# Long convolution: inputs turned by VectorE in 32x32 blocks, first input stage as products on 32x64 tiles

## The chip, the cores and the metric

The kernel runs on one core of a Trainium2 chip. The metric is the device time of one execution in microseconds (us). Engines are named as in the profile: PE is TensorE (PEld its weight loads), DVE is VectorE, ACT is ScalarE, POOL is GpSimd, SP is SyncE.

## The reference

Two blocks over a sequence of 2048 tokens with 1024 channels. The first is banded attention with multi-scale pooling. The second mixes a gated long convolution (changed here) with a spatial gating unit:

```
def second_block(x, ...):
    h = rms_norm(x, pre_norm_w); proj = h @ w_in
    hy_in, hy_gate, sg_u, sg_v, sg_gate = split(proj)
    x0, x1, v = split(short_conv_centred(hy_in, conv_w, conv_b))
    k = hyena_filter(L, ...)                      # (2L, 1024), divided by its l1 norm
    y_a = x0 * long_conv_bidir(v * x1, k, hyena_skip) * silu(hy_gate)
    ...
def long_conv_bidir(u, k, skip):
    U = rfft(u, n=2 * L, axis=1); K = rfft(k, axis=0)
    return irfft(U * K, n=2 * L, axis=1)[:, :L] + u * skip
```

Each channel's 2048 samples are thus convolved with a filter of 4096 taps and gated.

## The kernel before

The FFT of length 4096 is done in two stages of 64 points each, as matrix products, on two groups of 128 channels at a time: a chunk `cc` (four of them) is 256 channels, a group `ug` (eight) is 128 channels, `ug = 2*cc` or `2*cc + 1`. Everything lies in `long_convolution`, which is one program for each engine; the engines meet by semaphores alone, and each runs its instructions in the written order.

Filter: `generate(kq)` on PE makes 1/16 of a chunk's filter, `weighted(kq)` on DVE multiplies it by the decay, `absolute` (ACT) and `summed` (DVE) build the l1 norm. `filter_first(cc)` multiplies by the first-stage matrix in 16 groups, four PSUM banks in turn (0 to 3), and `filter_turned` (DVE) turns each out of PSUM.

Inputs: `channels_in(ug)` (SP) loads a group into UIN, channels on partitions, time along the row. Before, `inputs_turn(ug)` on PE transposes it in 16 steps of 128x128 into banks 0 and 1, `inputs_out(ug)` on ACT copies these to UI in four steps, and `inputs_first(ug)` on PE makes eight products of 128x128 by 512 columns, two for each of four groups of channels `g`, into banks 0 and 1 for even `g` and 2 and 3 for odd; `inputs_turned(ug)` on DVE turns them, 1024 columns at a time, into the buffer UB (`UTC`).

Loop: `second_stage(cc)` takes 16 steps `p`. In each, PE forms the second stage of filter and inputs, ACT copies the filter's form, DVE makes three products and a difference (the complex product), PE does `inverse(n)`, ACT writes it back into UB, and PE and DVE generate and weight a sixteenth of the next chunk's filter.

Boundary, between two loops: PE does `filter_first(cc+1)`, `inputs_turn(2cc+2)`, `inverse_first(2cc)`, `inputs_first(2cc+2)`, `inputs_turn(2cc+3)`, `inverse_first(2cc+1)`, `inputs_first(2cc+3)`. DVE does `filter_turned`, `outputs_turned` (2048 columns within SBUF for each of two halves of both groups), `norm`, `gate(2cc)`, `inputs_turned(2cc+2)`, `gate_product(2cc)`, `inputs_turned(2cc+3)`, `gate(2cc+1)`, `gate_product(2cc+1)`. `gate(ug)` adds the scaled result of `inverse_first`, from PSUM banks 4 to 7, to the buffer GU, which it walks at a stride of 32 words; `inverse_first(2cc+1)` waits bank by bank for `gate(2cc)`. `gate_product(ug)` multiplies GU by the gate.

GU is one buffer for all groups but the last. In SP's order, `gated_out(2cc)` waits for `ya_done` (set behind `gate_product(2cc)`) and stores GU; `gate_in(2cc+1)` waits until that is stored and loads the next group; ACT's `skip(2cc+1)` waits for the load and scales GU in place; and `gate(2cc+1)` waits for `skipped`. The lines are L2044, L2032, L2135 and L2260.

Of the kernel before, what the change touches and what calls it, by code (L numbers as in the profile page):

```python
# [1904 lines left out]
def long_convolution(nc, A, CC, HP, KX, M, PS, kept, L, gx_d, u_d, ya_d, yb_d):  # L1905

    with ExitStack() as ctx:
# [25 lines left out]
        AFU = region(41216, 2, P)  # L1933
# [16 lines left out]
        UIC = UI.rearrange("p (a c y) -> p c a y", a=8, y=2)  # L1950
        UIP = UI.rearrange("p (a c y) -> p a y c", a=8, y=2)
# [36 lines left out]
        utr_done = sem("utr_done")  # L1988
# [24 lines left out]
        def _(sp):  # L2013
# [8 lines left out]
            def channels_in(ug):  # L2022
                if ug:
                    sp.wait_ge(utr_done, 4 * ug)
                sp.dma_start(UIN, u_d[ug]).then_inc(uin_in, 16)

            def gate_in(ug):
                if ug == LAST:
                    sp.wait_ge(utr_done, 4 * LAST + 4)
# [18 lines left out]
            for dst, name in ((AF, "c_fwd"), (AFU.rearrange("p a b -> p (a b)"), "c_fwd_u"), (AI, "c_inv"),  # L2048
                              (SKIP, "hyena_skip_2"), (IDENT, "c_ident")):
                sp.dma_start(dst, A[name]).then_inc(const2_in, 16)  # L2050
# [47 lines left out]
        def _(s):  # L2098
# [22 lines left out]
            def inputs_out(ug):  # L2121
                for q in range(4):
                    n = 4 * ug + q
                    s.wait_ge(utr_done, n + 1)
                    if q == 0 and ug:
                        s.wait_ge(au_done, 8 * ug)
                    s.activation(UIP[:, 2 * q:2 * q + 2], PS[:, q % 2, :].rearrange("p (a y c) -> p a y c", a=2, y=2),
                                 ACT.Copy).then_inc(ui_done, 1)

# [17 lines left out]
            inputs_out(0)  # L2147
            inputs_out(1)
            for cc in range(NCH):
                for p in range(16):  # L2150
                    n = 16 * cc + p
                    bank, ks = banks_of(n)[0], KS[:, p % 3]
                    s.wait_ge(kf_done, n + 1)
                    if n >= 3:
                        s.wait_ge(pm_done, n - 2)
                    for to in range(2):
                        s.activation(ks[HID * to:HID * to + HID, 0], PS[0:HID, bank, :], ACT.Copy).then_inc(ks_done, 1)
                    for to in range(2):
                        s.activation(ks[HID * to:HID * to + HID, 1], PS[HID:P, bank, :], ACT.Copy,
                                     scale=1.0 - 2.0 * to).then_inc(ks_done, 1)  # L2160
                    if p == 0:
                        s.wait_ge(ks_done, ks_count(n) - 1)
                        s.activation(ks[0:1, 1, 0:CH], PS[HID:HID + 1, bank, 0:CH], ACT.Copy, scale=-1.0).then_inc(ks_done, 1)
                    if p >= lag_of(cc):
                        inverse_out(n - lag_of(cc))
                    if p:
                        if cc + 1 < NCH:
                            absolute(n + 15)
                        elif p in (12, 13):
                            s.wait_ge(au_done, 64)  # L2170
                            features_high(s, kept, L, p - 12, 1)
# [18 lines left out]
                inputs_out(2 * cc + 2)  # L2190
                inputs_out(2 * cc + 3)
# [3 lines left out]
        def _(v):  # L2195
# [32 lines left out]
            def inputs_turned(ug):  # L2228
                ct = ug % 2
                for g in range(4):  # L2230
                    n = 4 * ug + g
                    v.wait_ge(au_done, 2 * n + 2)
                    if g == 0 and ct == 0 and ug:
                        v.wait_ge(it_done, 2 * ug)
                    v.transpose(UTC[:, P * ct + 32 * g:P * ct + 32 * g + 32],
                                PS[:, 2 * (g % 2):2 * (g % 2) + 2, :].rearrange("p x (c i) -> p c x i", i=16)).then_inc(ut_done, 1)
# [39 lines left out]
            for kq in range(16):  # L2276
                weighted(kq)
                if kq > 1:
                    summed(kq - 2)
            filter_turned(0, range(0, 1))  # L2280
# [5 lines left out]
            inputs_turned(0)  # L2286
            inputs_turned(1)
            for cc in range(NCH):
                for p in range(16):
# [12 lines left out]
                    if cc + 1 < NCH:  # L2302
                        weighted(n + 16)
                        if p >= 2:
                            summed(n + 14)
                    elif p in (13, 14):
# [15 lines left out]
                if cc + 1 < NCH:  # L2322
# [9 lines left out]
                    norm(cc + 1)  # L2332
                outputs_turned(2 * cc + 1)
                gate(2 * cc)
                if cc + 1 < NCH:
                    inputs_turned(2 * cc + 2)
                gate_product(2 * cc)
                if cc + 1 < NCH:
                    inputs_turned(2 * cc + 3)
# [4 lines left out]
        def _(t):  # L2344
            h3 = H3.rearrange("p (m i) -> p i m", i=32)
            u16 = UIN.rearrange("p (k i) -> p i k", i=16)
# [23 lines left out]
            def filter_first(cc):  # L2370
                t.wait_ge(k_weighted, 16 * cc + 16)
                if cc:
                    t.wait_ge(pm_done, 16 * cc)
                for g in range(16):
# [15 lines left out]
            def inputs_turn(ug):  # L2390
                t.wait_ge(uin_in, 16 * (ug + 1))
                if ug % 2 == 0:
                    t.wait_ge(kt_done, 8 * ug + 16)
                else:
                    t.wait_ge(ut_done, 4 * ug - 1)
                for q in range(4):
                    n = 4 * ug + q
                    if q >= 2:
                        t.wait_ge(ui_done, n - 1)
                    for r in range(4):  # L2400
                        ins = t.transpose(PS[:, q % 2, P * r:P * r + P], u16[:, 4 * q + r], IDENT)
                    ins.then_inc(utr_done, 1)

            def inputs_first(ug):
                t.wait_ge(ui_done, 4 * ug + 4)
                for g in range(4):
                    n = 4 * ug + g
                    if g >= 2:
                        t.wait_ge(ut_done, n - 1)
                    elif g == 1 and ug % 2:  # L2410
                        t.wait_ge(ut_done, 4 * ug)
                    for x in range(2):
                        t.matmul(PS[:, 2 * (g % 2) + x, :], AFU[:, x], UIC[:, 32 * g:32 * g + 32],
                                 start=True, stop=True).then_inc(au_done, 1)
# [423 lines left out]
def constants():  # L2838
# [11 lines left out]
    c["c_fwd_u"] = np.zeros((P, 2, P), np.float32)  # L2850
    for x in range(2):
        c["c_fwd_u"][x::2, x] = c["c_fwd"][:HID]
    c["c_fwd_u"] = c["c_fwd_u"].reshape(P, 2 * P)
# [46 lines left out]
```

## Time and profile before

| | |
|---|---|
| median of three runs | 3109.48 us (3104.54 to 3125.76) |
| profiled execution, span | 3109.0 us |
| busy share PE / DVE / ACT | 96% / 81% / 27% |
| mean granted PE clock | 0.988 |
| long convolution | about 2229 to 2753 us of the span |

The span is the time from the first to the last instruction of one profiled execution, and serves as its own time. A clock of 1.00 is 2.4 GHz and 0.50 is 1.2 GHz. PE's busy time is modelled from pipelined records and overstates how near PE is to its peak. A timeline row merges like instructions, with the idle time before them and what ended it in brackets.

### The profile page before, as it was taken

Reading aid. Unit: us, or ns where it says so; the run is one execution under the profiler, and the core shown is the slowest. Engines: PE = TensorE matmul, PEld = TensorE weight load, DVE = VectorE, ACT = ScalarE, POOL = GpSimd, SP = SyncE. Lnnn points to the kernel's source line nnn. Section 1 sums busy time; section 2 is a strip of 40 time slices with the busy share of each in tenths; the row PEclk is TensorE's granted clock in tenths of the full one; section 3 lists DMA queues with packets and bytes.
Section 4 is the critical chain, followed back from the end, with each engine's and each line's share of the span. In section 5 each row is a group of like instructions: output and inputs, shape, how many; then the busy total and the mean of one; then the engine's idle time right before and its main releaser. Section 6 shows DMA issues by size and latency. Waiting matters only on the chain. (4 is left out here: it accounts for less than half of the span.)

```text
span 3109.0 us, 33058 instructions
## 1 busy us (share of the span) xinstructions
PE 2981.2 (96%) x12866; PEld 2164.2 (70%) x12866; DVE 2530.3 (81%) x2792; ACT 827.0 (27%) x1403; POOL 341.2 (11%) x466
## 2 busy tenths in 40 slices
PE   8999999999998999999999999999899999889999
PEld 4444444656776888888888888887656666678887
DVE  7979999898996869999999999999477979862221
ACT  3000000596334330000011111111443735631111
POOL 2211121001343430000000000000000100000000
PEclk9999999999999999999999999999999999999999
DMA  7576553301457545655654455551222331454231
GB/s 216 178 174 162 169 151 86 116 1 59 143 173 249 151 143 151 177 170 146 166 140 136 125 151 141 140 139 39 108 90 82 111 122 41 149 176 125 86 109 41
DMA packets 212244, 406.40 MB, mean 131 GB/s; under 512 B 21136, under 2 KB 134456, under 8 KB 204216
## 3 DMA queue, kind: packets, MB, share of 16 engines
q1 hardware_dynamic: 189256, 324.58, 34.5%
q0 software_dynamic: 21680, 71.32, 8.6%
q10 hardware_dynamic: 1152, 8.39, 0.7%
q8 instruction: 102, 1.67, 0.2%
q14 instruction: 54, 0.44, 0.0%
HBM read 324.53 MB, written 85.98 MB: 132 GB/s over the span
## 5 line engine op out<-in xcount | busy, mean ns | idle before, releaser
L1875 PE MATMUL PS<-HX,WH 128*128 128x512 f32 x1536 | 599.5, 390 | 6.9 <-DVE MB L1755 5.0
L1876 PE MATMUL PS<-HX,WH 128*128 128x512 f32 x1536 | 598.3, 390 | 0.0
L1877 PE MATMUL PS<-HX,WL 128*128 128x512 f32 x1536 | 598.3, 390 | 0.0
L849 PE MATMUL PS<-M 128*128 128x512 f32 x1088 | 471.2, 595 | 9.6 <-DVE M L650 8.3
L849 PEld LDWEIGHTS PS<-M 128*128 128x128 f32 x1088 | 207.2, 191 | 273.4 <-issue 263.0
L1875 PEld LDWEIGHTS PS<-HX,WH 128*128 128x128 f32 x1536 | 288.9, 188 | 67.8 <-DVE MB L1755 5.9
L1877 PEld LDWEIGHTS PS<-HX,WL 128*128 128x128 f32 x1536 | 288.8, 188 | 60.2
L1876 PEld LDWEIGHTS PS<-HX,WH 128*128 128x128 f32 x1536 | 289.0, 188 | 59.7
L120 DVE SCALAR_TENSOR_TENSOR HP<-MF,HP 128x1024 f32<-128x1024 f32 x252 | 323.5, 1284 | 8.0
L120 DVE SCALAR_TENSOR_TENSOR M<-M 128x1024 f32<-128x1024 f32 x160 | 205.6, 1285 | 26.9 <-DMA M<-c_feat 21.4
L2568 PE MATMUL PS<-WH,YH 128*128 128x512 f32 x512 | 202.1, 395 | 8.8 <-DVE HP L2707 5.2
L2569 PE MATMUL PS<-WH,YL 128*128 128x512 f32 x512 | 201.1, 393 | 0.0
L2570 PE MATMUL PS<-WL,YH 128*128 128x512 f32 x512 | 200.9, 392 | 0.0
L2691 DVE TENSOR_TENSOR YL<-KX,YH 128x2048 fp32r<-128x2048 f32 x14 | 32.1, 2292 | 206.8 <-ACT YH L2670 206.8
L1727 ACT ACTIVATE MB<-PS,MF 128x2048 f32<-128x2048 f32 x23 | 47.5, 2067 | 424.9 <-PE PS L1877 424.9
L2095 POOL DMA_DIRECT2D M<-c_decay x48 | 25.8, 538 | 1083.7 <-DVE KX L2209 885.2
L72 POOL DMA_DIRECT2D M<-c_feat x186 | 94.9, 515 | 382.9 <-DVE M L120 362.2
L2568 PEld LDWEIGHTS PS<-WH,YH 128*128 128x128 f32 x512 | 97.3, 190 | 31.1 <-issue 7.1
L1530 PE MATMUL PS<-WVH,HX 128*128 128x512 f32 x256 | 101.6, 397 | 14.4 <-DVE HX L1454 6.0
L1028 DVE TENSOR_TENSOR M<-M 128x1024 f32<-128x1024 f32 x90 | 110.1, 1223 | 2.4
L2569 PEld LDWEIGHTS PS<-WH,YL 128*128 128x128 f32 x512 | 97.4, 190 | 20.3
L2570 PEld LDWEIGHTS PS<-WL,YH 128*128 128x128 f32 x512 | 97.3, 190 | 20.5
(228 smaller groups left out, 5068.8 us busy)
## 6 DMA issues: line engine op xcount, KB each, us to landing
MF<-h_scratch SPq DMA_DIRECT2D x380, 256.0 KB, 4.3
M<-c_feat POOLq DMA_DIRECT2D x186, 256.0 KB, 4.3
MF<-w_in SPq DMA_DIRECT2D x52, 512.0 KB, 4.8
M<-u_scratch SPq DMA_DIRECT2D x16, 1024.0 KB, 4.8
M<-c_decay POOLq DMA_DIRECT2D x48, 256.0 KB, 2.9
M<-x SPq DMA_DIRECT2D x18, 512.0 KB, 4.1
M<-w_in SPq DMA_DIRECT2D x18, 512.0 KB, 4.7
x_scratch<-M SPq DMA_DIRECT2D x16, 512.0 KB, 5.0
```

The lines of the kernel that those rows point to most:

```text
L72: eng.dma_start(dst[HID * half:HID * half + HID], row).then_inc(loaded, 16)
L120: return v.scalar_tensor_tensor(out=out, in0=a, scalar=s_, in1=b, op0=op0, op1=op1)
L849: ins = t.matmul(ps[:, c, :], wt[:, k], HT[:, k, TC * c:TC * c + TC], start=(k == 0), stop=(k == KD - 1))
L1028: link(v.tensor_tensor(out, a, b, op))
L1530: t.matmul(dst, hh, wh, start=(k == 0), stop=False)
L1727: s.activation(AB[CONV_AT[kind]], ps, ACT.Identity, bias=w[:, 3:4], scale=w[:, 1:2]).then_inc(evac_done, 1)
L1875: t.matmul(dst, wh, hh, start=(k == 0), stop=False)
L1876: t.matmul(dst, wh, hl, start=False, stop=False)
L1877: ins = t.matmul(dst, wl, hh, start=False, stop=(k == KD - 1))
L2568: t.matmul(dst, yh, wh, start=(n == 0), stop=False)
L2569: t.matmul(dst, yl, wh, start=False, stop=False)
L2570: return t.matmul(dst, yh, wl, start=False, stop=(n == KY - 1))
```

## The change

PE's transposes (`inputs_turn`) and ACT's copies (`inputs_out`) are gone. A new DVE step `inputs_split(ug)` turns UIN into UI in 32x32 blocks in one instruction of 2048 columns; it reads along a stride of 64 words and writes along a stride of 16. In UI, each band of 32 partitions then holds 32 points of time for 32 channels. `inputs_first(ug, pair)` makes the first stage of two channel groups `g` as eight products with 32 rows, 64 output columns and 512 moving columns, one tile for each band and half (`side`), into all of banks 0 to 3. Each pair waits for the two turns of the pair before it. The constant `c_fwd_u` shrinks to 128x64.

The order moves too. For groups 0 and 1 the work goes into filter generation. For later chunks the even group's split stands at step 8 of the loop before, the odd group's behind `inputs_turned(2cc+2, 1)` in the boundary, and both turns of the odd group stand ahead of `gate_product(2cc)`. UIN is loaded again when a split has read it (`ui_done`) and no longer when PE has transposed it.

```diff
-        UIC = UI.rearrange("p (a c y) -> p c a y", a=8, y=2)
-        UIP = UI.rearrange("p (a c y) -> p a y c", a=8, y=2)
+        UIN_BLOCKS = UIN.rearrange("p (n t) -> p t n", t=64)
+        UI_BLOCKS = UI.rearrange("p (q c i) -> p q i c", c=32, i=16)
...
             def channels_in(ug):
                 if ug:
-                    sp.wait_ge(utr_done, 4 * ug)
+                    sp.wait_ge(ui_done, ug)
...
                 skip(2 * cc)
-                inputs_out(2 * cc + 2)
-                inputs_out(2 * cc + 3)
                 skip(2 * cc + 1)
...
+            def inputs_split(ug):
+                v.wait_ge(uin_in, 16 * (ug + 1))
+                if ug:
+                    v.wait_ge(au_done, 2 * ug)
+                v.transpose(UI_BLOCKS, UIN_BLOCKS).then_inc(ui_done, 1)
+
+            def inputs_turned(ug, pair):
                 ct = ug % 2
...
+                v.wait_ge(au_done, 2 * ug + pair + 1)
+                if ug >= 2:
+                    v.wait_ge(it_done, 2 * ug - 2)
+                for g in (2 * pair, 2 * pair + 1):
                     v.transpose(UTC[:, P * ct + 32 * g:P * ct + 32 * g + 32],
                                 PS[:, 2 * (g % 2):2 * (g % 2) + 2, :].rearrange("p x (c i) -> p c x i", i=16)).then_inc(ut_done, 1)
...
                 if kq > 1:
                     summed(kq - 2)
+                if kq == 5:
+                    inputs_split(0)
+                elif kq in (8, 11):
+                    inputs_turned(0, kq // 11)
+                if kq == 11:
+                    inputs_split(1)
+                elif kq == 14:
+                    inputs_turned(1, 0)
+            inputs_turned(1, 1)
             filter_turned(0, range(0, 1))
...
                             summed(n + 14)
+                        if p == 8:
+                            inputs_split(2 * cc + 2)
...
                     norm(cc + 1)
+                    inputs_turned(2 * cc + 2, 0)
                 outputs_turned(2 * cc + 1)
+                if cc + 1 < NCH:
+                    inputs_turned(2 * cc + 2, 1)
+                    inputs_split(2 * cc + 3)
                 gate(2 * cc)
                 if cc + 1 < NCH:
-                    inputs_turned(2 * cc + 2)
+                    inputs_turned(2 * cc + 3, 0)
+                    inputs_turned(2 * cc + 3, 1)
                 gate_product(2 * cc)
-                if cc + 1 < NCH:
-                    inputs_turned(2 * cc + 3)
                 gate(2 * cc + 1)
                 gate_product(2 * cc + 1)
...
+                else:
+                    t.wait_ge(ut_done, 8)
...
+            def inputs_first(ug, pair):
+                t.wait_ge(ui_done, ug + 1)
+                if pair or ug:
+                    t.wait_ge(ut_done, 4 * ug + 2 * pair)
+                if pair == 0 and ug >= 2 and ug % 2 == 0:
                     t.wait_ge(kt_done, 8 * ug + 16)
...
+                for x in range(2):
+                    for g in (2 * pair, 2 * pair + 1):
+                        rows = slice(32 * g, 32 * g + 32)
+                        for side in range(2):
+                            at = 1024 * side + 512 * x
+                            ins = t.matmul(PS[HID * side:HID * side + HID, 2 * (g % 2) + x, :], AFU[rows], UI[rows, at:at + 512],
+                                           start=True, stop=True)
+                ins.then_inc(au_done, 1)
...
             for kq in range(16):
                 generate(kq)
-            t.wait_ge(const2_in, 16 * 5)
+                if kq == 8:
+                    t.wait_ge(const2_in, 16 * 5)
+                    inputs_first(0, 0)
+                elif kq == 11:
+                    inputs_first(0, 1)
+                elif kq == 14:
+                    inputs_first(1, 0)
+            inputs_first(1, 1)
             filter_first(0)
-            inputs_turn(0)
-            inputs_first(0)
-            inputs_turn(1)
-            inputs_first(1)
...
                 if cc + 1 < NCH:
                     filter_first(cc + 1)
-                    inputs_turn(2 * cc + 2)
+                    inputs_first(2 * cc + 2, 0)
                 inverse_first(2 * cc)
                 if cc + 1 < NCH:
-                    inputs_first(2 * cc + 2)
-                    inputs_turn(2 * cc + 3)
+                    inputs_first(2 * cc + 2, 1)
+                    inputs_first(2 * cc + 3, 0)
                 inverse_first(2 * cc + 1)
                 if cc + 1 < NCH:
-                    inputs_first(2 * cc + 3)
+                    inputs_first(2 * cc + 3, 1)
...
-    c["c_fwd_u"] = np.zeros((P, 2, P), np.float32)
...
+    c["c_fwd_u"] = np.tile(c["c_fwd"][0:HID:2, 0:HID], (4, 1))
```

## Rows read from the trace of the kernel before

**Rows 1.** The page, part 1: busy time, share of the span, instructions.

```profile
PE 2981.2 (96%) x12866; PEld 2164.2 (70%) x12866; DVE 2530.3 (81%) x2792; ACT 827.0 (27%) x1403; POOL 341.2 (11%) x466
```

**Rows 2.** Busy time of each engine by stage; then granted PE clock, DMA share, GB/s.

```profile
2254.00:2269.00 15.00, 14.93 (x41) 6.99 (x41) 12.63 (x20) 0.63 (x1) 0.54 (x1) 1.00 0.11 33
2269.00:2291.40 22.40, 18.99 (x64) 9.89 (x65) 10.32 (x11) 4.59 (x8) 0.00 (x0) 1.00 0.53 194
...
2295.50:2358.90 63.40, 60.15 (x303) 42.63 (x302) 60.94 (x93) 50.98 (x90) 8.36 (x16) 0.99 0.21 63
2358.90:2419.60 60.70, 56.73 (x265) 37.25 (x264) 43.98 (x47) 15.01 (x21) 0.24 (x1) 0.98 0.21 74
```

**Rows 3.** The chain of waits where the convolution ends: start, length, what (us).

```profile
2758.53 5.42 DMA KX<-ya_scratch
```

**Rows 4.** DVE's timeline of the first boundary: start, length, instruction, idle before it.

```profile
2377.11 4.49 DVE L2243 STREAM_TRANSPOSE KX<-M 128x2048 f32<-128x2048 f32 x2
2381.69 1.21 DVE L2260 SCALAR_TENSOR_TENSOR M<-PS,M 128x512 f32<-128x512 f32 x1
...
2389.05 1.25 DVE L2235 STREAM_TRANSPOSE M<-PS 128x1024 f32<-128x1024 f32 x1 [0.57 <-PE PS L2413]
...
2395.46 2.32 DVE L2272 TENSOR_TENSOR M<-M 128x1024 f32<-128x1024 f32 x2
2406.00 1.25 DVE L2235 STREAM_TRANSPOSE M<-PS 128x1024 f32<-128x1024 f32 x1 [8.21 <-PE PS L2413]
...
2412.41 4.53 DVE L2260 SCALAR_TENSOR_TENSOR M<-PS,M 128x512 f32<-128x512 f32 x4
2416.97 2.36 DVE L2272 TENSOR_TENSOR M<-M 128x1024 f32<-128x1024 f32 x2
2419.57 0.69 DVE L2296 TENSOR_TENSOR M<-PS,M 128x512 f32<-128x512 f32 x1 [0.24 <-DVE M L2272]
```

**Rows 5.** DVE's timeline where the third and the fourth loop start.

```profile
2544.52 0.69 DVE L2296 TENSOR_TENSOR M<-PS,M 128x512 f32<-128x512 f32 x1 [0.24 <-DVE M L2272]
...
2669.94 0.69 DVE L2296 TENSOR_TENSOR M<-PS,M 128x512 f32<-128x512 f32 x1 [0.24 <-DVE M L2272]
```

**Rows 6.** PE's timeline of the same boundary.

```profile
2379.56 7.65 PE L2468 MATMUL PS<-M,KX 128*128 128x64 f32 x64
2387.04 7.21 PE L2413 MATMUL PS<-M 128*128 128x512 f32 x16
```

**Rows 7.** The sync engine's DMA queue in the same boundary.

```profile
2397.87 0.32 SPq L2044 DMA_DIRECT2D ya_scratch<-M  x1
2403.07 0.32 SPq L2032 DMA_DIRECT2D M<-u_scratch  x1
```

**Rows 8.** ScalarE's timeline of the same boundary.

```profile
2407.72 2.01 ACT L2135 ACTIVATE M<-M 128x2048 f32<-128x2048 f32 x1 [10.36 <-DMA M<-u_scratch]
```

**Rows 9.** Who waited for whom, 2229 to 2753: total us, times, longest.

```profile
ACT M L2135 <- DMA M<-u_scratch: 31.4, 3, 10.5
```

**Rows 10.** DVE groups by shape, whole span: busy us, mean ns, idle before.

```profile
L2260 DVE SCALAR_TENSOR_TENSOR M<-PS,M 128x512 f32<-128x512 f32 x32 | 37.6, 1213 | 11.0 <-PE PS L2468 11.0
...
L2209 DVE TENSOR_TENSOR M<-PS,M 128x512 f32<-128x512 f32 x32 | 21.9, 685 | 0.3 <-PE PS L2366 0.3
...
L2243 DVE STREAM_TRANSPOSE M<-M 128x2048 f32<-128x2048 f32 x8 | 18.0, 2282 | 0.0
```

**Rows 11.** PE's timeline at the filter's third layer (64x64 tiles).

```profile
2148.34 1.97 PE L1859 MATMUL PS<-MF 64*64 64x512 f32 x16
```

**Rows 12.** DVE's timeline in filter generation.

```profile
2253.11 0.69 DVE L2209 TENSOR_TENSOR KX<-PS,M 128x512 f32<-128x512 f32 x1 [0.30 <-ACT M L2105]
```

**Rows 13.** DMA issues of the prologue: KB each, us to landing.

```profile
M<-c_fft SPq DMA_DIRECT2D x1, 4096.0 KB, 14.2
```

**Rows 14.** Two stretches at the lower clock, columns as in rows 2.

```profile
2229.00:2233.00 4.00, 4.00 (x20) 2.47 (x22) 1.05 (x3) 3.96 (x8) 0.00 (x0) 0.50 0.68 270
2357.80:2361.20 3.40, 3.40 (x6) 2.08 (x7) 1.11 (x2) 2.00 (x3) 0.54 (x1) 0.51 0.33 83
```

More of the change, by code:

```diff
@@ L1932, in long_convolution @@
         AF = region(41088, P)
-        AFU = region(41216, 2, P)
+        AFU = region(41216, HID)
         AI = region(41472, HID)
@@ L1987, in long_convolution @@
         uin_in = sem("uin_in")
-        utr_done = sem("utr_done")
         ui_done = sem("ui_done")
@@ L2028, in gate_in @@
                 if ug == LAST:
-                    sp.wait_ge(utr_done, 4 * LAST + 4)
+                    sp.wait_ge(ui_done, LAST + 1)
                 elif ug:
@@ L2047, in _ @@
             channels_in(0)
-            for dst, name in ((AF, "c_fwd"), (AFU.rearrange("p a b -> p (a b)"), "c_fwd_u"), (AI, "c_inv"),
+            for dst, name in ((AF, "c_fwd"), (AFU, "c_fwd_u"), (AI, "c_inv"),
                               (SKIP, "hyena_skip_2"), (IDENT, "c_ident")):
@@ L2119, in absolute @@
                     s.activation(KABS[j % 2], out, ACT.Abs).then_inc(kabs_done, 1)
[L2121 to L2128, printed above, removed]
             def skip(ug):
@@ L2146, in _ @@
             s.wait_ge(const2_in, 16 * 5)
-            inputs_out(0)
-            inputs_out(1)
             for cc in range(NCH):
@@ L2169, in _ @@
                         elif p in (12, 13):
-                            s.wait_ge(au_done, 64)
+                            s.wait_ge(au_done, 16)
                             features_high(s, kept, L, p - 12, 1)
@@ L2226, in filter_turned @@
                     v.transpose(KTC[cc % 2][:, 16 * g:16 * g + 16], PS[:, n % 4, :]).then_inc(kt_done, 1)
-            def inputs_turned(ug):
-                ct = ug % 2
[L2230 to L2234, printed above, removed]
+            def inputs_split(ug):
[4 more added lines that the diff above has]
+            def inputs_turned(ug, pair):
+                ct = ug % 2
+                v.wait_ge(au_done, 2 * ug + pair + 1)
+                if ug >= 2:
+                    v.wait_ge(it_done, 2 * ug - 2)
+                for g in (2 * pair, 2 * pair + 1):
                     v.transpose(UTC[:, P * ct + 32 * g:P * ct + 32 * g + 32],
@@ L2285, in _ @@
             norm(0)
-            inputs_turned(0)
-            inputs_turned(1)
             for cc in range(NCH):
@@ L2345, in _ @@
             h3 = H3.rearrange("p (m i) -> p i m", i=32)
-            u16 = UIN.rearrange("p (k i) -> p i k", i=16)
             def generate(kq):
@@ L2388, in filter_first @@
                 ins.then_inc(l1_done, 1)
-            def inputs_turn(ug):
-                t.wait_ge(uin_in, 16 * (ug + 1))
-                if ug % 2 == 0:
-                    t.wait_ge(kt_done, 8 * ug + 16)
[L2394 to L2414, printed above, removed]
+            def inputs_first(ug, pair):
[3 more added lines that the diff above has]
+                if pair == 0 and ug >= 2 and ug % 2 == 0:
+                    t.wait_ge(kt_done, 8 * ug + 16)
+                for x in range(2):
[6 more added lines that the diff above has]
+                ins.then_inc(au_done, 1)
             def inverse(n):
@@ L2849, in constants @@
     c["c_fwd"], c["c_inv"], c["c_fft"] = fft_constants()
-    c["c_fwd_u"] = np.zeros((P, 2, P), np.float32)
-    for x in range(2):
-        c["c_fwd_u"][x::2, x] = c["c_fwd"][:HID]
-    c["c_fwd_u"] = c["c_fwd_u"].reshape(P, 2 * P)
+    c["c_fwd_u"] = np.tile(c["c_fwd"][0:HID:2, 0:HID], (4, 1))
     d, m, i = np.meshgrid(np.arange(2), np.arange(64), np.arange(32), indexing="ij")
```

## The prediction

> **What bounds the kernel now.** The page of the profile first: PE is busy for 96% of the span [rows 1]. That figure says nothing of the stretch that is changed, so I cut the span by stage [rows 2]. The convolution starts at 2229 us; the chain of waits that ended last passes from its stored result, read back at 2758.5 us, into the output stage [rows 3]. So a shift of the convolution's end should move the end of the kernel one for one. I take that as the rule below.
>
> Within the convolution there are four kinds of stretch [rows 2]. Behind filter generation, the filter's first stage takes 15 us, the inputs' first stage 22.4 us; then come four loops of 16 steps (63.4 us for the first, in which DVE is busy 60.9) with a boundary after each of the first three (60.7 us for the first, DVE busy 44.0). The loop is DVE's: 63.4 / 16 = 3.96 us a step, nearly all of it DVE work. The boundary is a ping-pong between PE and DVE. Next comes DVE's timeline of the first boundary [rows 4]: it ends when the next loop's first product starts at 2419.57. The other two boundaries repeat it (the third and fourth loop start at 2544.52 and 2669.94 [rows 5], cycles of 125.0 and 125.4 us). PE's timeline beside it [rows 6] gives what each PE block costs: 7.65 us for `inverse_first`, 7.21 us for the old `inputs_first`.
>
> One thing is easy to miss: GU is a single buffer. After `gate_product(2cc)` it is stored, the next channel group is loaded into it, ScalarE scales it (`skip`), and only then can `gate(2cc+1)` run. In the first boundary the product ends at 2395.46 + 2.32 = 2397.78 [rows 4], the store is issued at 2397.87 and the load at 2403.07 [rows 7], the scaling runs from 2407.72 to 2409.73 [rows 8]. That is a **turn-round of 11.95 us**; ScalarE waited on this load in three places, 31.4 us in all [rows 9]. Today it costs nothing: the second group's turned inputs lie between the product and the second gate, which starts at 2412.41 [rows 4], 2.7 us after the scaling is done.
>
> **The change part by part.**
>
> *First, the new DVE turn* (`inputs_split`, eight in all). Its price is not in the trace. It turns 128x2048 fp32 within SBUF, reading single words 256 B apart and writing them 64 B apart. The existing turn of that size takes 2.27 us [rows 4, 10], but it moves pairs of adjacent words. The only DVE work here that walks single words at a long stride is the gate (128 B): 1213 ns for 512 columns, where a DVE product from PSUM of the same size at a stride of 8 B takes 685 ns [rows 10]. The excess is 0.53 us per 512 elements, 2.11 us for 2048. So the bounds are 2.27 us (stride free) and 2.27 + 2 x 2.11 = 6.5 us (read and write each pay). I take T = 2.27 + 2.11 = 4.4 us, since the gate too is strided on both sides and pays once. The Trainium skill ("SBUF — State Buffer", Door 1: The DMA port swizzle, the note on cachelines) says that full bandwidth needs two hits in each 16-byte line, so that four-byte words each in its own line pay and pairs do not. By that rule the time is that of A below, by the plain turn's rows alone that of B.
>
> *Second, the products on 32x64 tiles* (`inputs_first(ug, pair)`): eight products of 512 columns, on four different tiles. The nearest row is the filter's third layer: eight 64x64 products of 512 columns on four tiles, 16 records in 1.97 us [rows 11]. Eight full-array ones take 7.21 us [rows 6], so four run side by side. I take 2.0 us per pair, 4.0 per group. The bounds are 1.97 and 3.6 (only the row halves overlap). The four PSUM turns of a group stay at 1.25 us each [rows 4], and since each pair now fills all four banks, its products wait for the last pair's turns: PE and DVE alternate where they overlapped before. The Trainium skill ("TensorEngine Tiling (Array Packing)", Performance Considerations, PSUM Bottleneck) warns of this: tiling does not speed up the evacuation of PSUM. Without it one would book 3.2 us of gain for each of the six groups turned in boundaries, some 19 us in all.
>
> *Third, the prologue.* The 22.4 us between the filter's stage and the second stage go away: -22.4. In exchange DVE gets, inside and after generation, two splits (2 x 4.4 = 8.8), four pairs of PSUM turns (4 x 2.42 = 9.7, from 1.25 plus a 1.17 spacing), and about 1.0 of waiting round the last pair. DVE is idle only 0.30 us in every second step of generation, released by ScalarE's decays [rows 12], and ScalarE waits on DVE in turn, so it can hide about 1.0 of it. The sum is -22.4 + 8.8 + 9.7 + 1.0 - 1.0 = **-3.9 us**. Removing ScalarE's evacuations frees ScalarE, which bounds nothing here. The tables for the second stage take 14.2 us to land [rows 13]; issued as generation begins, they are there well ahead of need. The queue's loads of UIN now wait for a split instead of PE's turning; each is issued a loop earlier and delays nothing behind it, by my reading.
>
> *Fourth, each loop* before a boundary gets one split at step 8. DVE has no slack there [rows 2]: +4.4 us.
>
> *Fifth, each boundary*, worked in the first one's times. DVE's norm ends and PE's filter stage frees the banks at 2377.0. PE: pair (2,0) until 2379.0; DVE turns it 2379.1 to 2381.5, then the second half of the outputs (4.49) until 2386.0. PE's `inverse_first(0)` (7.5 to the next block) ends at 2386.5, pair (2,1) at 2388.5; DVE turns it until 2391.0 and splits until 2395.4. The gate (4.5) ends at 2399.9, the turn of (3,0) at 2402.4. PE: pair (3,0) until 2397.4, `inverse_first(1)` until 2404.9, pair (3,1) until 2406.9 (it wants the turn of (3,0), long done); DVE turns that until 2409.4. Only now comes `gate_product(0)`, until 2411.8. Nothing lies any more between it and `gate(1)`, which waits for the turn-round: 2411.8 + 11.95 = 2423.7. Gate 4.53, product 2.36, and the loop's first product starts at 2430.9 instead of 2419.57: **+11.3 us**. Without the turn-round it would be 2418.9, a gain of 0.7: the freed PE time is there, but what lies behind it is the buffer's way through memory.
>
> *Sixth, the clock.* When PE takes up the convolution it runs at half its clock (granted 0.50, so 1.2 GHz, for 2229 to 2233), and at the head of the first boundary it was 0.51 again, though PE had hardly paused [rows 14]. The change leaves PE idle some 7 us during the split and the gap before it, and 14 us in the turn-round. DVE hides most: I estimate +1.5 per boundary and +0.5 in the prologue, 5 in all (bounds 0 and 12).
>
> **The sum** against the profiled execution (span 3109.0, the same as the median of three, 3109.48, which spread from 3104.5 to 3125.8): 3 x (4.4 + 11.3) - 3.9 + 5 = 47.1 - 3.9 + 5 = +48.2, so **3157 us**.
>
> **The rivals.** (A) The forecast, 0.55, with 3148 to 3168 as its own range. (B) The strided turn costs nothing extra, T = 2.3. Then a loop gets 2.3 and a boundary 9.2, the prologue is -8.1, the clock 3: 34.5 - 8.1 + 3 = +29, 3138 us. For it: the existing strided turn at full rate; against it: that one moves pairs. 0.18. (C) The 32x64 tiles overlap only two at a time, 1.6 us more per pair: four pairs on the boundary's chain, three boundaries, and 3 in the prologue, +22 on A: 3179 us. Against it stands the third layer's 1.97 us; 0.09. (D) The other side, no slower at all: the turn-round is covered. The mechanism is the slot between `gate_product(2cc)` and `gate(2cc+1)`; it decides from the point at which store, load and scaling take less than what lies between, which is now nothing. If the scaled input were there, and T = 2.3, a boundary would be 2.8 shorter and its loop 2.3 longer: 3 x -0.5 - 8.1 = -10, 3099 us. For it speaks only that the store took 5.2 us of the 11.95 while half of a gate was being fetched beside it, so a store alone might be quicker; against it, the three waits of ScalarE on exactly this load. 0.08. (E) T near 6.5, or more of the clock's bound: 3 x (6.5 + 13.4) + 0.3 + 8 = +68, 3177 us; 0.10. That the change does not do what it says (ScalarE and PE still turning inputs) I see no place for in the code.
>
> **How the numbers follow.** The likeliest is A, 3157. The range goes from 3129, the low end of B, to 3180, the top of C and E. Leaving out D and the tails, it holds about 0.85. About 1% (31 us) is what a measurement of this kernel tells from no change. Slower by more than that (over 3140) are A, C, E and a quarter of B, less a little for a median that wanders by half a per cent: 0.72. Within 1%: most of B and of D, 0.25. Faster by more: 0.03.
>
> **What the profile of the changed kernel would show.** The split's row near 4.4 us (2.3 means B, 6.5 means E). Each pair of the inputs' first stage 2.0 us on PE (3.6 means C). In DVE's timeline of each boundary, an idle stretch of about 12 us before the second gate, released by ScalarE's scaling, which waits for the load of GU; its absence means D and makes the forecast wrong by the most. The second stage starting right behind the filter's first, some 4 us earlier than before; loop starts about 140 us apart against 124 to 125. Loops of 68 us for the first three and an unchanged last.

## The result and the profile after

The changed kernel takes 3207.88 us (3203.57 to 3207.96) against 3109.48: a ratio of 1.0291, with a 95% interval from 1.0264 to 1.0318. The profiled execution spans 3206.1 us, 97.1 more than before. It is slower, as forecast, but by twice the forecast 48.

Where the 97.1 us lie is read from the starts of the convolution and of the four loops on DVE. The convolution starts at 2230.8 (before 2229.0: 1.8 us of spread in the parts ahead of it, which are the same code), the first loop at 2300.7 (before 2295.5, so 3.3 more for the prologue), and the fourth at 2768.1 against 2669.9 [rows 5]. The three cycles of loop and boundary take 155.1, 157.7 and 154.7 us where they took 124.0, 125.0 and 125.4: 93.0 us more, 31.0 each. What follows the fourth loop's start is 1.1 us shorter. By stage, the table that answers to [rows 2] (generation with the inputs' first stage inside it, the filter's first stage, the first loop, the first boundary, and 50 us of that boundary alone); the number after the counts is the granted clock:

```profile
2230.80:2278.80 48.00, 35.49 (x193) 15.79 (x193) 34.56 (x40) 23.77 (x49) 2.19 (x4) 0.68 0.64 246
2278.80:2296.50 17.70, 17.68 (x40) 8.03 (x41) 12.62 (x18) 0.00 (x0) 0.00 (x0) 0.84 0.03 13
2300.70:2368.80 68.10, 61.62 (x305) 43.01 (x302) 64.66 (x94) 50.99 (x90) 8.35 (x16) 0.97 0.25 74
2368.80:2455.80 87.00, 63.93 (x258) 42.45 (x257) 45.88 (x48) 10.05 (x13) 0.27 (x1) 0.64 0.11 40
2387.00:2437.00 50.00, 41.40 (x185) 31.67 (x182) 23.66 (x17) 0.00 (x0) 0.00 (x0) 0.50 0.00 1
```

The loop grew from 63.4 to 68.1 us. The boundary grew from 60.7 to 87.0, and its clock, 0.98 before, is 0.64; from 2387 to 2437 it is 0.50, that is 1.2 GHz, though PE is busy for 41 of those 50 us. The other two boundaries are alike: from 2544 to 2594 and from 2701 to 2751 the granted clock is 0.50 too, with PE busy for 41.4 us each time. DVE's timeline of the first boundary, the answer to [rows 4]:

```profile
2387.63 2.38 DVE L2226 STREAM_TRANSPOSE M<-PS 128x1024 f32<-128x1024 f32 x2 [2.15 <-PE PS L2405]
2389.94 4.46 DVE L2234 STREAM_TRANSPOSE KX<-M 128x2048 f32<-128x2048 f32 x2
2405.12 2.38 DVE L2226 STREAM_TRANSPOSE M<-PS 128x1024 f32<-128x1024 f32 x2 [10.72 <-PE PS L2405]
2407.43 3.58 DVE L2218 STREAM_TRANSPOSE M<-M 128x2048 f32<-128x2048 f32 x1
2410.91 4.19 DVE L2251 SCALAR_TENSOR_TENSOR M<-PS,M 128x512 f32<-128x512 f32 x4
2415.03 2.36 DVE L2226 STREAM_TRANSPOSE M<-PS 128x1024 f32<-128x1024 f32 x2
2432.29 2.38 DVE L2226 STREAM_TRANSPOSE M<-PS 128x1024 f32<-128x1024 f32 x2 [14.90 <-PE PS L2405]
2434.59 2.32 DVE L2263 TENSOR_TENSOR M<-M 128x1024 f32<-128x1024 f32 x2
2448.94 4.21 DVE L2251 SCALAR_TENSOR_TENSOR M<-PS,M 128x512 f32<-128x512 f32 x4 [12.03 <-ACT M L2125]
2453.18 2.36 DVE L2263 TENSOR_TENSOR M<-M 128x1024 f32<-128x1024 f32 x2
2455.79 0.69 DVE L2294 TENSOR_TENSOR M<-PS,M 128x512 f32<-128x512 f32 x1 [0.24 <-DVE M L2263]
```

Two idle stretches, of 10.7 and 14.9 us, end on PE; the third, 12.03 us ahead of the second gate, ends on ACT. PE's timeline shows what the first two waited for (answer to [rows 6]):

```profile
2385.32 2.27 PE L2405 MATMUL PS<-M 32*64 32x512 f32 x16 [0.51 <-DVE M L2212]
2387.52 13.92 PE L2461 MATMUL PS<-M,KX 128*128 128x64 f32 x64
2401.36 3.69 PE L2405 MATMUL PS<-M 32*64 32x512 f32 x16
2411.06 3.69 PE L2405 MATMUL PS<-M 32*64 32x512 f32 x16 [6.01 <-DVE M L2218]
2414.68 13.92 PE L2461 MATMUL PS<-M,KX 128*128 128x64 f32 x64
2428.53 3.69 PE L2405 MATMUL PS<-M 32*64 32x512 f32 x16
```

`inverse_first` takes 13.92 us twice where it took 7.65, from the same instructions, and a pair of the new products takes 3.69 us. The one pair that straddles the fall of the clock, at 2385.3, takes 2.27. The clock rises again at 2438, in the second stage's first products (128x128 weights, 256 columns), which start at 2434.8, and falls once more while PE stands idle behind the turn-round. The queue and ACT behind the third stretch (answers to [rows 7, 8]):

```profile
2437.00 0.32 SPq L2043 DMA_DIRECT2D ya_scratch<-M  x1
2442.07 0.32 SPq L2031 DMA_DIRECT2D M<-u_scratch  x1
```

```profile
2446.85 2.00 ACT L2125 ACTIVATE M<-M 128x2048 f32<-128x2048 f32 x1 [74.88 <-DMA M<-u_scratch]
```

From the product's end (2434.59 + 2.32 = 2436.91) to the end of the scaling (2448.85) it is 11.94 us. The split's row, busy and mean (answer to the last of [rows 10]):

```profile
L2218 DVE STREAM_TRANSPOSE M<-M 128x2048 f32<-128x2048 f32 x8 | 29.7, 3716 | 0.0
```

The prologue on PE: the same 16 records once at 1.2 and once at 2.4 GHz, and the filter's first stage behind them:

```profile
2247.68 3.69 PE L2405 MATMUL PS<-M 32*64 32x512 f32 x16
...
2255.51 1.95 PE L2405 MATMUL PS<-M 32*64 32x512 f32 x16
...
2278.77 16.88 PE L2382 MATMUL PS<-KX,M 128*128 128x512 f32 x32 [2.58 <-DVE M L2226]
```

### The profile page after: what moved, and what is told of

It reads as the page before. It is cut to its first block and busy times, and to the rows that moved or that the text cites. A ratio compares the mean times of both kernels' runs of the same rounds, so it can differ in the third digit from the quotient of the medians.

```text
span 3206.1 us, 33051 instructions
## 1 busy us (share of the span) xinstructions
PE 3016.1 (94%) x12866; PEld 2182.3 (68%) x12866; DVE 2553.3 (80%) x2800; ACT 808.0 (25%) x1371; POOL 341.5 (11%) x466
## 5 line engine op out<-in xcount | busy, mean ns | idle before, releaser
L2435 PE MATMUL PS<-M 128*128 128x256 f32 x384 | 109.2, 424 | 18.6 <-DVE M L2251 12.4
```

The costliest lines, as they stand in the source:

```text
L2435: ins = t.matmul(PS[:, bank, CH * x:CH * x + CH], STRIP[:, 2 * p + x], src[:, p, x], start=True, stop=True)
```

## The experiments

Three questions: does the turn-round cost by itself, what is it that holds the clock down, and what does the split cost. All times are medians but those of experiment 7. The kernel before, run beside them, stood at 3112.5 us for experiments 1, 3, 4 and the first of 6, at 3107.4 for 5, 7 and 8, and at 3111.1 for 2, the second of 6, and 9. The changed kernel's 3207.9 was taken beside 3109.5, so differences of a few us between these times say nothing.

**1. The gate's product ahead of the odd group's turns** (`product_early`).

```diff
-                    inputs_turned(2 * cc + 3, 0)
-                    inputs_turned(2 * cc + 3, 1)
-                gate_product(2 * cc)
+                    gate_product(2 * cc)
+                    inputs_turned(2 * cc + 3, 0)
+                    inputs_turned(2 * cc + 3, 1)
                 gate(2 * cc + 1)
```

> The changed kernel with gate_product(2cc) put back behind gate(2cc), ahead of both turns of the odd group; nothing else is different. Theory 1 (GU's turn-round is what the boundary ends on): the idle stretch of 12.0 us ahead of the second gate goes, because the PE work at the lower clock now lies inside it; the second gate then waits only for the last turn. By the changed kernel's rows the next loop would start about 14 us earlier in each of three boundaries, so 3207.9 - 43 = 3165 us. Theory 2 (the clock alone is the cause, and the turn-round is only hidden idle): the gain is under 15 us, because PE stays at 1.2 GHz and something else on its chain ends as late.

3166.1 us, ratio 1.0164 (1.0123 to 1.0205): 41.8 us less than the changed kernel. Its DVE timeline shows the second gate directly behind the last turn, with no wait; the idle time before that turn, 12.2 us, is PE at the low clock:

```profile
2430.11 2.38 DVE L2226 STREAM_TRANSPOSE M<-PS 128x1024 f32<-128x1024 f32 x2 [12.21 <-PE PS L2405]
2432.41 4.49 DVE L2251 SCALAR_TENSOR_TENSOR M<-PS,M 128x512 f32<-128x512 f32 x4
```

Theory 1 holds. The granted clock is 0.51 for 2386 to 2437 here too, so this edit leaves the other cost untouched.

**2. The same exposure in the kernel before** (`before_late`).

```diff
-                gate_product(2 * cc)
                 if cc + 1 < NCH:
                     inputs_turned(2 * cc + 3)
+                gate_product(2 * cc)
                 gate(2 * cc + 1)
```

> The kernel before with one line moved: gate_product(2cc) stands behind inputs_turned(2cc+3), as in the changed kernel; nothing of the turns, the tiles or the clock is touched. Theory 1 (the turn-round of GU costs by itself): the product ends at 2414.7 in the first boundary instead of 2397.8, the second gate waits 12 us for the scaled input, the loop starts 14.3 us later; three boundaries, 3109 + 43 = 3152 us. Theory 2 (the wait only shows because PE was slow or the clock low): under 10 us more, below 3120.

3148.8 us, ratio 1.0117 (1.0086 to 1.0148). One moved line costs 38 us in a kernel whose turns and tiles are those of before:

```profile
2410.43 2.32 DVE L2272 TENSOR_TENSOR M<-M 128x1024 f32<-128x1024 f32 x2
2424.71 4.27 DVE L2260 SCALAR_TENSOR_TENSOR M<-PS,M 128x512 f32<-128x512 f32 x4 [11.96 <-ACT M L2135]
...
2431.62 0.69 DVE L2296 TENSOR_TENSOR M<-PS,M 128x512 f32<-128x512 f32 x1 [0.24 <-DVE M L2272]
```

The product ends at 2412.75, the second gate starts 11.96 us later, and the next loop starts at 2431.6 instead of 2419.6. That is 12.0 us where 14.3 were expected: this boundary also began 2.0 us sooner (its first turn of the filter at 2359.6 against 2361.6), since PE was not at its low clock there. The other two cycles grew by 13.2 and 11.5 us. Both `inverse_first` of this boundary take 7.65 us, as in the kernel before, so the clock has no part in it. Theory 1 holds.

**3. Fillers** (`fill`). Six products of the full array in each boundary, into banks whose next real product overwrites them.

```diff
+            def fill(count, bank):
+                for _ in range(count):
+                    t.matmul(PS[:, bank, :], AF, region(0, 512), start=True, stop=True)
             def inputs_first(ug, pair):
+                if pair == 0 and ug >= 2 and ug % 2:
+                    t.wait_ge(ut_done, 4 * ug)
+                    fill(4, 0)
...
                     inputs_first(2 * cc + 2, 0)
+                    fill(2, 4)
                 inverse_first(2 * cc)
```

> The changed kernel with six products of the full array, 512 columns each, added in every boundary, whose results are overwritten unread: two between pair (2cc+2, 0) and inverse_first(2cc), four while PE waits for the split of group 2cc+3. Theory 1 (clock): they keep the granted clock at 1.0, inverse_first takes 7.6 us instead of 13.9 twice a boundary, pairs 2.0 instead of 3.7; less 2 us for the fillers on the chain, some 14 us gained a boundary, so about 3165 us. Theory 2 (the 32x64 tiles or the alternation with VectorE make the blocks slow by themselves): blocks stay at 13.9 and 3.7 us and the kernel is 6 to 20 us slower, 3214 to 3228 us.

3171.9 us, ratio 1.0181 (1.0132 to 1.0229): 36 us less than the changed kernel, although PE does more. PE's timeline, with the filler (L2396), `inverse_first` and a pair:

```profile
2389.27 3.30 PE L2396 MATMUL PS<-M 128*128 128x512 f32 x4
2392.41 7.64 PE L2468 MATMUL PS<-M,KX 128*128 128x64 f32 x64
2399.98 1.95 PE L2412 MATMUL PS<-M 32*64 32x512 f32 x16
```

7.64 and 1.95 us: what was slow in the changed kernel was the clock and not the tile or the alternation. The fillers do not keep the clock from falling, they bring it back: it falls at the same place (the pair ahead of them takes 2.28 us, and the granted clock is 0.50 from 2389 to 2391) and is up again when `inverse_first` starts. Theory 1 holds; its size was 7 us too optimistic.

**4. The same products on 128 rows by 64 columns** (`rows128`). The weights of each band of 32 rows are padded with zeros to 128, so only two products run side by side, where the 32x64 tiles let four, and a pair has to take longer.

```diff
-                            ins = t.matmul(PS[...], AFU[rows], UI[rows, at:at + 512],
+                            ins = t.matmul(PS[...], AFU[:, g], UI[:, at:at + 512],
...
-    c["c_fwd_u"] = np.tile(c["c_fwd"][0:HID:2, 0:HID], (4, 1))
+    c["c_fwd_u"] = np.zeros((P, 4, HID), np.float32)
+    for g in range(4):
+        c["c_fwd_u"][32 * g:32 * g + 32, g] = c["c_fwd"][0:HID:2, 0:HID]
```

> The changed kernel with the first input stage as products of all 128 rows on 64 columns: the weights of each band are padded with zeros to 128 rows, the rest is the same. Only two of these run side by side, so each pair should take 3.6 us at 2.4 GHz where the 32x64 tiles take 2.0. Theory 1 (the time over the forecast is PE's clock, granted 0.50 from the first 32x64 pair of a boundary on, and fuller use of the array keeps it up): the clock stays at 1.0 through most of each boundary, inverse_first takes 7.6 us instead of 13.9, and in spite of slower pairs the kernel is faster, about 3172 us. Theory 2 (the lower clock comes from PE's waits, whatever the tile): the clock stays low, pairs take over 5 us and the kernel is slower than the changed one, 3225 to 3245 us.

3183.2 us, ratio 1.0222 (1.0181 to 1.0263), 25 us less than with the tiles. In its first boundary, the pair behind 7.75 us of `inverse_first` takes 3.65 us; the next one, begun after 6 us without work, starts at the low clock (5.85) and ends at the high one, so that the second `inverse_first` takes 7.75 again. Theory 1 holds; its size was 11 us too optimistic:

```profile
2391.51 7.75 PE L2460 MATMUL PS<-M,KX 128*128 128x64 f32 x64
2399.19 3.65 PE L2404 MATMUL PS<-M 128*64 128x512 f32 x16
2408.84 5.85 PE L2404 MATMUL PS<-M 128*64 128x512 f32 x16 [5.99 <-DVE M L2218]
2414.61 7.75 PE L2460 MATMUL PS<-M,KX 128*128 128x64 f32 x64
```

**5. The tiles, twice over** (`tiles_twice`). This separates "PE had too little to do" from "this kind of work does not count for much".

```diff
-                for x in range(2):
+                for x in (0, 1, 0, 1):
```

> The changed kernel with each pair's eight 32x64 products made twice over with the same result. At 2.4 GHz a pair then takes 3.7 us, as on 128 rows. Theory 1 (what brings the clock back is the time that PE spends in 512-column products, on whatever tile): the clock is as in the variant on 128 rows and the time too, about 3183 us. Theory 2 (work on 32-row tiles does little for the clock, however long it lasts): the clock stays at 0.50 through the boundaries as in the changed kernel, pairs take 7.2 us, and the kernel is slower than the changed one by three pairs on the path of each boundary and some of the prologue's, about 3207.9 + 3 x 10 + 8 = 3246 us.

3256.7 us, ratio 1.0463 (1.0434 to 1.0493). The doubled pairs take 7.10 us, as long as the old `inputs_first`, and the clock stays at 0.50 through 64 us in which PE is busy for 55:

```profile
2401.00:2465.00 64.00, 55.39 (x248) 36.11 (x241) 23.73 (x17) 0.00 (x0) 0.00 (x0) 0.50 0.02 5
```

```profile
2404.13 13.91 PE L2461 MATMUL PS<-M,KX 128*128 128x64 f32 x64
2417.98 7.10 PE L2405 MATMUL PS<-M 32*64 32x512 f32 x32
```

Theory 2 holds. It was 11 us short because I had booked three of a boundary's four pairs and all four got longer (the first 5.61 us instead of 2.27); in the profiled execution, at 3262.2 us the longest of the four, the cycles grew by 17.0, 13.7 and 13.6 us and the prologue by 11.1, where 8 had been booked. PE's time on these tiles did not bring the clock back here; in runs 3 and 4 it rose during the fillers and during the padded products.

**6. Both cures together** (`early_rows128`, `early_fill`): the edit of run 1 on top of run 4, and on top of run 3.

> Both edits: the product ahead of the odd group's turns, and the products on 128 rows by 64 columns. Theory 1 with the clock up: the turn-round lies behind PE's work at full speed, the next loop starts some 4 us later than in the kernel before, the loop is 3.7 us longer, so three times 7 to 8 us and a prologue about even: 3130 us. If the clock stays low here too, the first edit's gain is all there is, 3165 to 3190 us.

> The changed kernel with both cures that leave its 32x64 tiles: gate_product ahead of the odd group's turns, and six full-array products a boundary whose results are overwritten. If turn-round and clock are two separate costs, the gains add up but for what the turn-round hid: from the rows of the filled variant the second gate starts at 2426.6 instead of 2438.1, so 11.4 us a boundary less than there: 3172 - 34 = 3138 us. If they are one and the same cost, it stays near 3165.

3143.3 us, ratio 1.0092 (1.0060 to 1.0124), and 3138.7 us, ratio 1.0084 (1.0055 to 1.0114). The first is 13 us over what was expected: its three cycles are 11.2, 7.8 and 7.5 us longer than before where 7 to 8 were booked, and its prologue, booked as even, is 3.3 us longer. For the second the sum was right within a microsecond: turn-round (41.8) and fillers (36.0) take 69.2 us together, so they are two costs, with 8.6 us of overlap. In `early_fill` the second gate still waits 3.1 us, since PE is now quick enough to end inside the turn-round. The trace names no releaser for that wait ("issue"); ACT's row shows it, the scaling that ends at 2421.53:

```profile
2416.11 2.38 DVE L2226 STREAM_TRANSPOSE M<-PS 128x1024 f32<-128x1024 f32 x2 [4.12 <-PE PS L2412]
2421.62 4.53 DVE L2251 SCALAR_TENSOR_TENSOR M<-PS,M 128x512 f32<-128x512 f32 x4 [3.13 <-issue]
```

```profile
2419.53 2.00 ACT L2125 ACTIVATE M<-M 128x2048 f32<-128x2048 f32 x1 [51.03 <-DMA M<-u_scratch]
```

**7. What the strides cost** (`read_plain`, `write_plain`). Each takes away one of the split's two strides; the inputs are then placed wrongly, which changes no other instruction.

```diff
-        UIN_BLOCKS = UIN.rearrange("p (n t) -> p t n", t=64)
+        UIN_BLOCKS = UIN.rearrange("p (t n) -> p t n", t=64)
```

```diff
-        UI_BLOCKS = UI.rearrange("p (q c i) -> p q i c", c=32, i=16)
+        UI_BLOCKS = UI.rearrange("p (q i c) -> p q i c", c=32, i=16)
```

> The split reads adjacent words (the blocks of UIN are taken in another order, so the convolution's inputs are wrongly placed) and still writes words 64 B apart. It took 3.72 us with both strided. If the read's stride of 256 B is what costs, it falls to 2.3 us; if the write's, it stays at 3.7; if each has a share, it lies between.

> The other half: the split reads words 256 B apart and writes adjacent words (again the inputs are wrongly placed). 3.7 us if the read's stride is what costs, 2.3 us if the write's.

The split's row, read in order first, then written in order:

```profile
L2218 DVE STREAM_TRANSPOSE M<-M 128x2048 f32<-128x2048 f32 x8 | 29.0, 3619 | 0.0
```

```profile
L2218 DVE STREAM_TRANSPOSE M<-M 128x2048 f32<-128x2048 f32 x8 | 29.3, 3657 | 0.0
```

3.62 and 3.66 us, against 3.72 with both strides and 2.28 for the turn that moves pairs. None of the outcomes that I had written down for one guilty side: either stride alone costs nearly all of the 1.4 us, and the two do not add. The whole kernels took 3197.5 and 3201.2 us, one run each, which says nothing more.

**8. The replacement in the order of before** (`replaced`). Products on 128 rows for one group of channels at a time, banks alternating as before; the product at once behind its gate; both splits in the boundary, none in the loop. PE's order is again `filter_first`, `inverse_first(2cc)`, `inputs_first(2cc+2)`, `inverse_first(2cc+1)`, `inputs_first(2cc+3)`; in the prologue only split 0 lies in generation, the rest behind the filter's stage.

```diff
-                    inputs_turned(2 * cc + 2, 0)
-                outputs_turned(2 * cc + 1)
-                if cc + 1 < NCH:
-                    inputs_turned(2 * cc + 2, 1)
-                    inputs_split(2 * cc + 3)
+                    inputs_split(2 * cc + 2)
                 gate(2 * cc)
-                if cc + 1 < NCH:
-                    inputs_turned(2 * cc + 3, 0)
-                    inputs_turned(2 * cc + 3, 1)
                 gate_product(2 * cc)
+                inputs_turned(2 * cc + 2, (0, 1))
+                outputs_turned(2 * cc + 1, (0,))
+                inputs_turned(2 * cc + 2, (2, 3))
+                outputs_turned(2 * cc + 1, (1,))
+                inputs_split(2 * cc + 3)
                 gate(2 * cc + 1)
+                inputs_turned(2 * cc + 3)
                 gate_product(2 * cc + 1)
```

> VectorE's split and the products on 128 rows by 64 columns, in the order of the kernel before: groups of 32 channels alternate between two pairs of banks, so products and turns overlap; gate_product(2cc) follows its gate at once; both splits stand in the boundary where VectorE has idle time, none in the loop; in the prologue only split 0 lies in generation. Theory 1 (what the change lost lies in order, clock and turn-round, not in the split itself): the loop is back at 63.4 us, the boundary about 2 us shorter than before, the prologue within 2 us of before, no second gate waits for scaling: 3100 to 3112 us, the same as before. Theory 2 (the split's 3.7 us cannot be hidden, because VectorE is on the path in the boundary too): two splits a boundary show in full, 3109 + 22 = 3131 us.

3138.7 us, ratio 1.0096 (1.0080 to 1.0113). It looks like Theory 2, and it is not: PE's timeline has the clock again.

```profile
2374.61 12.27 PE L2452 MATMUL PS<-M,KX 128*128 128x64 f32 x64 [0.62 <-DVE M L2239]
2386.81 8.84 PE L2396 MATMUL PS<-M 128*64 128x512 f32 x32
2400.17 13.66 PE L2452 MATMUL PS<-M,KX 128*128 128x64 f32 x64 [4.52 <-DVE KX L2234]
```

Both `inverse_first` run low for most of their length (12.27 and 13.66 us). The first starts at the high clock and loses it two microseconds in: it now follows the l1 products of one column at once, without the transposes that stood between them before. So it does in the other two boundaries (12.69 and 13.01 us). The second follows an idle 4.52 us.

**9. The same with fillers** (`replaced_fill`): `fill(2, 4)` ahead of `inverse_first(2 * cc)`, in the last chunk too, and `fill(4, 4)` ahead of `inverse_first(2 * cc + 1)`, behind a wait for `gate(2 * cc)`, whose banks it overwrites.

> The variant in the order of before (splits in the boundary, products on 128 rows by 64 columns), with two full-array products ahead of inverse_first(2cc) and four in PE's idle 4.5 us ahead of inverse_first(2cc+1), their results overwritten. There the clock had fallen at the head of both: 12.3 and 13.7 us instead of 7.7. Theory 1 (the rest of that variant's loss is clock): 4.6 + 5.9 us less, 1.8 us for the first two fillers, some 9 us a boundary, 3139 - 27 = 3112 us, the time of before or a little under. Theory 2 (VectorE's own work is now the path): under 3 us a boundary, above 3130.

3106.1 us (3102.4 to 3108.7) against 3111.1 for before: a ratio of 0.9978 (0.9960 to 0.9995). Clock and loop start:

```profile
2378.82 7.64 PE L2456 MATMUL PS<-M,KX 128*128 128x64 f32 x64
...
2399.36 7.75 PE L2456 MATMUL PS<-M,KX 128*128 128x64 f32 x64 [0.49 <-DVE KX L2234]
```

```profile
2419.69 0.69 DVE L2291 TENSOR_TENSOR M<-PS,M 128x512 f32<-128x512 f32 x1 [2.02 <-ACT M L2151]
```

`inverse_first` is back at 7.64 and 7.75 us, and the first cycle takes 121.9 us (2297.8 to 2419.7) where it took 124.0. So 33 us of the last variant's time were clock (35.7 between the three cycles of the two profiled executions), more than the 27 expected. Theory 1 holds, and VectorE's split, well placed, costs about what PE's and ScalarE's turning did. This kernel has fillers and the kernel before has none, so the comparison is not of the turning alone; the kernel before was not run with fillers. The interval lies just under one, but a gain of 0.2% is within what I had called no change.

## Why the prediction was wrong

*The turn-round of GU* was right, in its mechanism and its size: 11.95 us read from before, 11.94 in the changed kernel, and a wait of 12.03 at the second gate, released by the scaling. Run 2 shows it in the old code, run 1 takes it away. Rival D, that it would be covered, is out.

*The sixth step, the clock, is the one that failed.* It had the right sign and the wrong size by a factor of ten: 1.5 us a boundary, with a bound of 12 us for the whole kernel. In the first boundary the two `inverse_first` lost 12.5 us and three pairs 5.1, 17.6 us on PE's chain, for which I had booked 1.5 and "DVE hides most". DVE hid little of it: the boundary grew by 26.3 us, of which the turn-round was to be 11.3, and DVE stood idle for 10.7 and 14.9 us while PE worked. The error lay in how I pictured it. I tied the low clock to PE's idle stretches, which DVE's work covers, and let it recover behind each. In fact it fell while PE was working, at the end of the first 32x64 pair and so just ahead of the first `inverse_first`, behind the one-column l1 products and half a microsecond of wait; and nothing that followed for 50 us brought it back, neither products of 64 columns nor those on tiles. Runs 3 and 5 settle that: it rose during full-array products, and twice as many tile products left it low. Rival E held "more of the clock's bound", which was the right direction, but stopped at 3177.

What had held the clock up before is shown only in part. Ahead of the first `inverse_first` stood 16 transposes of 128x128, which the change takes away:

```profile
2377.03 1.14 PE L2401 MATMUL PS<-M 128*128 128x128 f32 x8 [0.52 <-DVE M L2226]
2378.45 1.27 PE L2401 MATMUL PS<-M 128*128 128x128 f32 x8 [0.28 <-ACT M L2127]
```

With them the granted clock was 1.00 from 2377 to 2404; in the second and third boundary of the kernel before it fell in this place too, from 2502 to 2504 and from 2628 to 2630, and was up again early in `inverse_first`, whose two blocks there took 7.70 and 8.44 us. Without them, in run 8, it fell in all three boundaries and stayed low through the rest of the block. The full-array `inputs_first` of 7.21 us stands behind the first `inverse_first` and can't have helped it; it can have helped the second. Neither it nor the transposes were taken out of the kernel before by themselves, so the share of each is argued.

Booking 17.6 us gives 3157 + 3 x 16.1 = 3205, against 3207.9, but that closeness is partly luck. The three cycles would then be 3 x (4.4 + 11.3 + 17.6) = 99.9 us longer and were 93.0; the 7 us too many there are offset by 7 us too few in the prologue.

*The prologue* came to +3.3 us, not -3.9 (-3.4 with the clock's 0.5). Generation with the inputs' stage in it took 48.0 us instead of 25.0, the filter's stage 17.7 instead of 15.0, and the 22.4 us behind them went: 23.0 + 2.7 - 22.4 = 3.3. The rows point to the clock: pairs of 3.69 us instead of 2.0 in three of four cases, for which DVE waits 2.2, 2.2 and 2.7 us, and a filter stage of 16.88 us where PE needed 14.1 at the high clock. No run isolates it. In `rows128` the filter's stage is back at 14.11 us, but its pairs take 3.65 to 5.52 us, and the prologue stays at 70.7 us, against 69.9; so for the prologue the cause is argued, not shown.

*The new turn* was priced at 4.4 us and took 3.72. That an access of single words at a long stride costs extra was right, and rival B is out; the note on cachelines in the Trainium skill ("SBUF — State Buffer", Door 1: The DMA port swizzle) points the same way, without a size, and the trace agrees: 3.72 us against 2.28 for the turn that moves pairs. The size was taken from the gate, whose excess does not carry over: the split pays 1.4 us for 2048 elements and not 2.1, and as run 7 shows once, whichever side is strided. The loop's +4.4 came out as +4.7, of which 3.7 is the split.

*The tiles* were right at the clock for which they were priced: 1.95 us a pair against 2.0 forecast. Rival C is out as a fact of the tiles. But a tile block has two prices, and the other one, 3.69, is what the boundary paid. The turns out of PSUM stayed as long as they were booked, 2.38 us a pair against 2.42, while a pair of products shrank to 1.95 at the high clock; so the warning that the prediction took from the Trainium skill ("TensorEngine Tiling (Array Packing)", Performance Considerations, PSUM Bottleneck), that tiling does not speed up the evacuation, held.

*The range* ended at 3180, and the clock's bound of 12 us under it had no working. The rows beside it were two stretches of about 4 us. The kernel before had a longer one, which the prediction leaves out: near the end of the fourth loop, from 2717 to 2726, the granted clock was 0.50 with PE busy for 7.1 of the 9 us. Even that is short of the 50 us that came.

## What to carry to other kernels

Before you move work off a busy engine's line, list what the removed blocks did besides their own work: here full-array transposes and products stood between the blocks of 64-column products, and with them gone TensorE ran at 1.2 GHz and code that the change does not touch took 13.9 us instead of 7.65. A product that is faster by tiling may be dearer in total than a padded one (3207.9 us against 3183.2 here); try the padded form, or a few fillers in idle slots (3171.9). And where a single buffer goes out to memory and comes back, what stands between its release and its next use is cover: count it before moving anything out.

## What was not expected of the hardware

The granted clock stayed at 0.50 for 50 us in which PE was busy for 41, and for 64 us in `tiles_twice` with PE busy for 55. The blocks on it were products with 64 moving columns behind a full weight load each, and products on 32x64 tiles. Both ran at the high clock too: behind fillers, padded products or the full-array work of the kernel before, the 64-column block went through at 2.4 GHz in 7.65 to 7.75 us. In run 8 it started at the high clock behind one-column products and lost it on the way (12.27 us), and behind the low clock it took 13.9. So the same block takes 7.7 to 13.9 us according to what ran ahead of it. Why these blocks left the clock low where others raised it, no run here separates. Strided single words on one side of a VectorE turn cost 1.34 to 1.38 us per 2048 elements, on both sides 1.44; the two sides do not add.
